# Block 0's expert numbers worked out on GpSimd, two heads at a time, with the gathers queued behind the pairs

## The reference

```python
def peer_rows(xb, w_pq, sub_keys, peer_u, peer_v):
    q = (xb @ w_pq).reshape(n, 8, 2, 128)
    s = jnp.einsum('nhcd,hckd->nhck', q, sub_keys)          # 8 heads x 2 halves x 128 keys
    top_s, top_i = lax.top_k(s, 16)
    cand_s = (top_s[:, :, 0, :, None] + top_s[:, :, 1, None, :])   # 256 sums per head
    cand_i = (top_i[:, :, 0, :, None] * 128 + top_i[:, :, 1, None, :])
    best_s, best_pos = lax.top_k(cand_s, 16)
    idx = jnp.take_along_axis(cand_i, best_pos, axis=-1)    # 16 expert rows per head
    g = jax.nn.softmax(best_s, axis=-1)
    a = jax.nn.gelu(jnp.einsum('nd,nhkd->nhk', xb, peer_u[idx]))
    return jnp.einsum('nhk,nhkd->nd', g * a, peer_v[idx])
```

## Time and profile before

| | |
|---|---|
| median of 3 runs | 2230.27 us (2228.47 to 2231.19) |
| profiled execution | 2234.23 us |
| its span | 2232.4 us |
| mean granted TensorE clock | 0.819 |
| TensorE matmul busy | 1487.6 us (67%) |
| VectorE busy | 1345.3 us (60%) |
| GpSimd busy | 1073.2 us (48%), 1126 instructions |
| ScalarE busy | 205.8 us (9%) |
| bytes moved | 748.24 MB, mean 335 GB/s |

### The profile page before, as it was taken

The page is one execution under the profiler, slowest core; times in us unless marked ns, Lnnn a source line. Parts: engine busy times, 40 slices in busy tenths (PEclk is TensorE's granted clock), DMA queues, the critical chain, the costliest instruction groups (busy, mean ns, idle before and its releaser), DMA issues.

```text
span 2232.4 us, 17911 instructions
## 1 busy us (share of the span) xinstructions
PE 1487.6 (67%) x6304; PEld 678.1 (30%) x6304; DVE 1345.3 (60%) x2853; ACT 205.8 (9%) x464; POOL 1073.2 (48%) x1126
## 2 busy tenths in 40 slices
PE   6989679988853334999923379995004995004998
PEld 3444443454641212443411123661001221001222
DVE  2778962244289775551479861476999934995001
ACT  3113300002100100001110001110000001000000
POOL 0411112110016565555545445557777777766773
PEclk9999789878876666999955599998556997556999
DMA  6777437736359998999989889999999999999997
GB/s 264 263 288 277 156 120 284 299 118 245 132 208 379 405 405 340 404 385 388 355 344 381 334 352 371 353 358 398 409 409 409 408 409 409 410 411 410 409 409 299
DMA packets 219113, 748.24 MB, mean 335 GB/s; under 512 B 20384, under 2 KB 25248, under 8 KB 208656
## 3 DMA queue, kind: packets, MB, share of 16 engines
q0 software_dynamic: 160368, 616.91, 70.9%
q1 hardware_dynamic: 50464, 121.24, 14.7%
q10 hardware_dynamic: 8192, 8.95, 1.1%
HBM read 736.98 MB, written 10.04 MB: 335 GB/s over the span
## 4 chain that ended last, share of the span: by engine, by line
PE 45%; DMA 24%; DVE 14%; POOL 9%; issue 6%; ACT 2%; ACTq 0%; SPq 0%; DVEq 0%; POOLq 0%
PE ps L1850 17%; DMA arena<-in_peer_u,arena 16%; PE ps L1633 15%; POOL arena L629 9%; DMA arena<-in_peer_v,arena 6%; DVE arena L1295 6%; PE ps L2022 4%; DVE arena L981 3%; DMA arena<-in_cache_diff_v,arena 1%; PE ps L1740 1%; PE ps L1637 1%; PE ps L1594 1%; PE ps L2012 1%; PE ps L1806 1%; PE ps L1798 1%
## 5 line engine op out<-in xcount | busy, mean ns | idle before, releaser
L629 POOL DMA_INDIRECT arena<-in_peer_u,arena x520 | 488.0, 938 | 450.7 <-DVE arena L1295 216.1
L1295 DVE CUSTOM_DVE_ANT_0 arena<-arena,ps 128x1024 f32<-128x1024 f32 x512 | 611.6, 1219 | 63.7 <-DMA arena<-in_peer_u,arena 48.3
L629 POOL DMA_INDIRECT arena<-in_peer_v,arena x520 | 495.7, 953 | 281.2 <-PE ps L1850 149.1
L1850 PE MATMUL ps<-arena 128*32 128x512 f32 x2048 | 557.7, 604 | 10.2 <-DMA arena<-in_peer_v,arena 5.3
L1633 PE MATMUL ps<-arena 128*128 128x512 f32 x960 | 440.0, 614 | 7.4 <-ACT arena L681 6.6
L1850 PEld LDWEIGHTS ps<-arena 128*32 128x32 f32 x2048 | 152.2, 110 | 382.7 <-issue 285.3
L1633 PEld LDWEIGHTS ps<-arena 128*128 128x128 f32 x960 | 184.0, 196 | 240.3 <-issue 229.8
L981 DVE TENSOR_TENSOR arena<-arena 128x256 f32<-128x256 f32 (+12 forms) x299 | 188.9, 667 | 28.7 <-ACT arena L964 8.6
L1841 PE MATMUL ps<-arena 128*128 128x128 f32 x4 | 1.6, 389 | 290.4 <-DVE arena L981 290.4
L981 DVE TENSOR_TENSOR arena<-arena,ps 128x512 f32<-128x512 f32 (+6 forms) x59 | 48.9, 831 | 213.1 <-PE ps L1633 77.0
L2022 PE MATMUL ps<-arena 128*128 128x128 f32 (+1 forms) x768 | 133.0, 330 | 2.2 <-ACT arena L681 1.4
(11 more groups left out here) (224 smaller groups left out, 1233.7 us busy)
## 6 DMA issues: line engine op xcount, KB each, us to landing
arena<-in_w_pq SPq DMA_DIRECT2D x12, 2048.0 KB, 18.8
arena<-in_w_in SPq DMA_DIRECT2D x7, 2048.0 KB, 10.9
arena<-in_w_out SPq DMA_DIRECT2D x6, 2048.0 KB, 14.8
arena<-in_w_mq SPq DMA_DIRECT2D x6, 2048.0 KB, 9.9
arena<-in_w_mo SPq DMA_DIRECT2D x6, 2048.0 KB, 19.5
arena<-in_peer_u,arena POOLq DMA_INDIRECT x520, 11.3
arena<-in_peer_v,arena POOLq DMA_INDIRECT x520, 14.1
arena<-in_cache_mem_k SPq DMA_DIRECT2D x8, 1024.0 KB, 7.0
```

The source lines that it names most:

```text
L629: return pool.indirect_dma_start(slot, None, table[0], bass.IndirectOffsetOnAxis(idx.bitcast(U32), 0))
L1295: dve.tensor_tensor_reduce(row, row, x_copy(b), 1.0, 0.0, ALU.mult, ALU.add, DOTS[:, k:k + 1]).then_inc(s["u_used"], 1)
L1850: last = pe.matmul(PS[32 * j:32 * j + 32, 6 + half, :], window(n, i, j), row[:, 512 * half:512 * half + 512], start=(n == 0 and i == 0), s ...
```

## The change

Only block 0 is concerned (`b == 0`); for the other blocks `select_heads` is as before. For block 0, VectorE stops behind the two comparisons. It writes the rows of 0 and 1 not to HOTS but to one of two buffers PAIR_HOTS in the ring, copies the pair's key numbers (64 per token) to PAIR_NUMBERS, and raises `heads_found`. From the third pair on it first waits for `picked`, so that GpSimd has done with the buffer.

GpSimd has a new function `pick_pair`: wait for `heads_found`; four multiplications; four additions that halve the 16 places to one (8, 4, 2, 1); times 128, plus the second number, and a conversion into IDX, which raises `picked` by two. Pair 0 is done before the first gather; pairs 1, 2 and 3 stand, one after another, behind the nine gathers that have a free place, and before the tenth. To make room for the two new semaphores, `new_kv_stored` and `state_stored` become one, `rows_and_state_stored`, and the wait for the state is at 16 x 10 + 16.

```diff
--- before.py
+++ after.py
@@ -268,19 +268,20 @@
...
-        mem_stored0 mem_stored1 mem_stored2 mem_stored3 new_kv_stored lam_sums lam_exp line_ps line_row
+        mem_stored0 mem_stored1 mem_stored2 mem_stored3 rows_and_state_stored lam_sums lam_exp line_ps line_row
...
@@ -452,6 +453,9 @@
         HOTS = at("t", 0, 1024)
         BV, BI, AU, CU = (at("t", 1024 + 32 * i, TOPK * HEADS) for i in range(4))
         GAC = at("t", 1296, 2 * TOPK * HEADS)
+        PAIR_HOTS = [at("ring", 1024 * i, 1024) for i in range(2)]
+        PAIR_NUMBERS = [at("t", 1360 + 64 * i, 2 * TOPK * HEADS) for i in range(2)]
+        PAIR_SUM = at("t", 1488, TOPK * HEADS)
         bsum, bmax = at("t", 1184, PH), at("t", 1192, PH)
         IDX = at("const", CW - NB * NSEL, NB * NSEL).rearrange("p (b k) -> p b k", b=NB)
         GATE = at("s", 320, NB * NSEL).rearrange("p (b k) -> p b k", b=NB)
@@ -631,12 +635,46 @@
 
             pool.wait_ge(s["mixed_turned"], NB - 1)
             pool.wait_ge(ns_stored[2], stored_through(2))
+            pool_links = [0]
+
+            def plink(ins):
+
+                pool_links[0] += 1
+                ins.then_inc(s["pool_steps"], 1)
+                pool.wait_ge(s["pool_steps"], pool_links[0])
+
+            def pick_pair(p):
+
+                wide = HEADS * TOPK
+                pool.wait_ge(s["heads_found"], p + 1)
+                hots = PAIR_HOTS[p % 2].rearrange("p (t h k a) -> p t h k a", t=2, h=HEADS, a=TOPK)
+                numbers = PAIR_NUMBERS[p % 2].rearrange("p (h t k) -> p h t k", h=HEADS, t=2)
+                for half in range(2):
+                    for h in range(HEADS):
+                        last = pool.tensor_tensor(hots[:, half, h], hots[:, half, h],
+                                                  numbers[:, h, half].unsqueeze(1).broadcast_to([P, TOPK, TOPK]), ALU.mult)
+                plink(last)
+                h3 = PAIR_HOTS[p % 2].rearrange("p (x a) -> p x a", a=TOPK)
+                n = TOPK // 2
+                while n:
+                    plink(pool.tensor_tensor(h3[:, :, 0:n], h3[:, :, 0:n], h3[:, :, n:2 * n], ALU.add))
+                    n //= 2
+                number = IDXF[:, wide * p:wide * p + wide]
+                plink(pool.tensor_scalar(PAIR_SUM, h3[:, 0:wide, 0], float(NK), None, ALU.mult))
+                plink(pool.tensor_tensor(number, PAIR_SUM, h3[:, wide:2 * wide, 0], ALU.add))
+                pool.tensor_copy(IDX[:, 0, wide * p:wide * p + wide].bitcast(U32), number).then_inc(s["picked"], HEADS)
+
             for kind, b, k0, k1 in RUNS:
                 if b == SMP and kind == "u":
                     pool.wait_ge(s["idxt_ready"], PICKS.index(SMP) + 1)
                 elif b != SMP and kind == "v":
                     pool.wait_ge(s["idxt_ready"], PICKS.index(b) + 1)
                 for k in range(k0, k1):
+                    if (kind, b, k) == ("u", 0, 0):
+                        pick_pair(0)
+                    if (kind, b, k) == ("u", 0, len(VSLOT)):
+                        for p in range(1, PH // HEADS):
+                            pick_pair(p)
                     slot, _, before = GATHERS[kind, b, k]
                     if not before and slot >= len(VSLOT):
                         pool.wait_ge(s["rqp_ready"], NSUB * LAST + (12 if slot < len(VSLOT) + 4 else 16))
@@ -738,7 +776,7 @@
                     j = first_job(kind) + b
                     take(j, dst[0:ROWS[b], b, :])
                     taken(j)
-                    act.dma_start(outs if b == SMP else outp[b], dst[0:ROWS[b], b, :]).then_inc(s["new_kv_stored"], 16)
+                    act.dma_start(outs if b == SMP else outp[b], dst[0:ROWS[b], b, :]).then_inc(s["rows_and_state_stored"], 16)
                     if kind == "dk" and b < H:
                         line_copy(b)
                 if kind == "dk":
@@ -750,7 +788,7 @@
                 act.dma_start(TOE[:, h, :], line_dram[o:o + P * (TL - 1)].rearrange("(p c) -> p c", p=P)[:, 0:512]
                               ).then_inc(s["toe_loaded"], 16)
 
-            act.wait_ge(s["new_kv_stored"], 16 * NSTORES)
+            act.wait_ge(s["rows_and_state_stored"], 16 * NSTORES)
             act.wait_ge(s["srow_saved"], 1)
             for st in range(NBLK * H + 2):
                 if st < NBLK * H:
@@ -792,7 +830,7 @@
                               SLOT[TILE_SLOT[n][0]][:, 0:512].rearrange("p (h e) -> p h e", h=H)).then_inc(ns_stored[TILE_SLOT[n][0]], 16)
             act.wait_ge(s["ret_state"], NBLK)
             act.dma_start(state_p[0, 0].rearrange("h d e -> d h e"), STATE.rearrange("p (h e) -> p h e", h=H)
-                          ).then_inc(s["state_stored"], 16)
+                          ).then_inc(s["rows_and_state_stored"], 16)
 
             def head_sqrt(n, b0, b1):
                 act.wait_ge(s["hsq_ready"], n + 1)
@@ -1145,7 +1183,7 @@
             link(tt(sself_m[0:DB], sself_m[0:DB], sself_e[0:DB], ALU.add))
             tt(colmax[0:DB, :].rearrange("p (b c) -> p b c", b=DB), colmax[0:DB, :].rearrange("p (b c) -> p b c", b=DB),
                sself_m[0:DB], ALU.max).then_inc(s["largest_ready"], 1)
-            dve.wait_ge(s["new_kv_stored"], 16 * NSTORES)
+            dve.wait_ge(s["rows_and_state_stored"], 16 * NSTORES)
             dve.wait_ge(s["av_done"], NBLK * H)
             turned_row("rq", 0, DV, 0)
 
@@ -1383,6 +1421,18 @@
                 dve.tensor_copy(GATE[0:r, b, h0 * TOPK:(h0 + HEADS) * TOPK], BV[0:r])
 
                 wide = HEADS * TOPK
+                if b == 0:
+                    p = h0 // HEADS
+                    if p >= 2:
+                        dve.wait_ge(s["picked"], HEADS * (p - 1))
+                    dve.tensor_copy(PAIR_NUMBERS[p % 2], TIFB[b][:, h0 * 32:(h0 + HEADS) * 32].bitcast(U32))
+                    for half, pos in enumerate((AU, CU)):
+                        last = tt(PAIR_HOTS[p % 2][:, 512 * half:512 * half + 512].rearrange("p (x a) -> p x a", a=TOPK),
+                                  pos.bitcast(U32).unsqueeze(2).broadcast_to([P, wide, TOPK]),
+                                  const("iota16").unsqueeze(1).broadcast_to([P, wide, TOPK]), ALU.is_equal)
+                    last.then_inc(s["heads_found"], 1)
+                    dve.wait_ge(s["heads_found"], p + 1)
+                    return
                 hots = [HOTS[0:r, 512 * half:512 * half + 512] for half in range(2)]
                 iota = const("iota16")[0:r].unsqueeze(1).broadcast_to([r, wide, TOPK])
                 for hot, pos in zip(hots, (AU, CU)):
@@ -1428,7 +1478,7 @@
             for g, blocks in enumerate(GROUPS):
                 prompt = [b for b in blocks if b != SMP]
                 if g == 0:
-                    dve.wait_ge(s["state_stored"], 16)
+                    dve.wait_ge(s["rows_and_state_stored"], 16 * NSTORES + 16)
                     head_norm(1, 1, NBLK, SQ)
                     dve.wait_ge(s["x_again"], 32)
                 residual("mix", g)
```

More of the change, by code:

```diff
@@ L275 @@
         ret_sc_ready ret_out ret_state ret_rows rqm_ready kexp_ready outer_ready ns_ready ns_stored0 ns_stored1
[L276 to L283, removed]
+        ns_stored2 hsq_ready hrstd_done mix_ready x_again done_stored final_ready mkr_loaded mkr_turned mkT_done
+        mv_loaded cs_ready cmax_ready cexp_done ce_turned ceT_ready co_ready co_taken cqb_ready cs_scored
+        ccolmax_turned cmaxbc_ready csexp_done cesum_ready cz_ready ccoef_ready cpv_done com_ready crow_ready
+        sk_loaded sk_turned skT_done rqp_ready rqp_taken rs_ready rs_taken xb_ready gelu_done weight_ready
+        y_ready u_used v_used select_steps picked idx_turned idxt_ready gate_arg gate_exp_done gates_done
+        w_turned wx_ready slot_in0 slot_in1 slot_in2 slot_in3 slot_in4 slot_in5 slot_in6 slot_in7 slot_in8
+        slot_in9 slot_in10 slot_in11 slot_in12 slot_in13 slot_in14 slot_in15 slot_in16 qdec_loaded sq_stored
+        qb_in0 qb_in1 mixed_turned mixed_done tile_in3 largest_ready clargest_ready x_in_ps heads_found
+        pool_steps""".split()
 def build(nc, x_prompt, x_sample, mem_prompt, cache_diff_k, cache_diff_v, page_table, state_ret, cache_mem_k,
```

## The result

The changed kernel takes 2217.85 us in the median of seven runs (2213.41 to 2224.75) against 2228.47 us before (median of seven; the forecast started from the first three, 2230.27, and said 2221.8): ratio 0.9951, interval 0.9937 to 0.9965. Measured again on the chip of the last experiments it took 2220.39 us, ratio 0.9959 (0.9943 to 0.9975). That is 10.6 and 9.1 us faster by the medians; forecast were 8.5. The profiled execution took 2216.49 us, its span is 2214.7 us, 17.7 less than before. Half of that lies ahead of the change: the fourth sort of block 0's router began at 600.03 instead of 609.00, and how much of it is more than scatter between executions stays open (first experiment).

What follows compares the result with a forecast made beforehand. No single engine was the bound; TensorE, DMA and VectorE shared the chain, with VectorE nearly full in block 0's selection. -11.9 + 3.5 = -8.4, taken as 8.5, off the 2230.27 median gave 2221.8 us; range 2215.5 to 2229.5.

Steps and rivals of the forecast that it cites:

- VectorE's path: Block 0's router and selection: 2.98 us net off VectorE per pair, four pairs, 11.9 us in all.
- rival 1: Block 0's router: TensorE keeps its clock, both stalls go, gain 11.7 or up to 14 us; chance 0.18.
- the first stall: VectorE's 1.62 us wait for TensorE's matmuls after pair 0; forecast to keep its size if the clock still falls.
- GpSimd's pair: GpSimd's eleven instructions with seven waits per pair in block 0, taken as 7.5 us between bounds 3.5 and 13.9.
- rival 3: Block 0's sorts, gates, first dot products: VectorE held while GpSimd computes; at half speed 6.5 us slower, 2237; chance 0.10.
- The lag behind pair 3: Tenth gather waits for GpSimd's pair 3, so gathers move 8.4 us, not 11.9; VectorE meets 3.5 us in full.
- The sum -11.9 + 3.5 = -8.4: Block 0's path: VectorE's shorter selection less the gathers' lag behind pair 3; 8.5 us gain taken.
- the collision: The DMA-limited stage behind selection: w_mq tiles move by 8.9 us, gathers by 8.4, so the full stretch begins that much earlier.
- The damping: Stage behind selection: with a 13.9 us pair, the second w_mq tile fills part of the gap; about 5 us gain left.
- X: GpSimd's time for one pair's arithmetic in block 0, forecast 7.5 us.

Runs made afterwards that it cites:

- the last experiments: Changed kernel with group 1's first w_mq tile issue held until VectorE's first dot product is done, 2224.05 us; changed kernel with pair 1 behind six gathers, 2219.53 us.
- first experiment: The kernel before with only the merged semaphore rows_and_state_stored added: 2230.43 us, ratio 1.0002.
- the seven traces with GpSimd's arithmetic: Changed kernel, profiled twice (2217.85, 2220.39 us), and its five variants: last pair on VectorE, last pair late, longer pair 3, w_mq held, pair 1 sooner (2219.53 to 2224.48 us).
- pair 3 late: Changed kernel with pair 3 moved behind 64 gathers in GpSimd's queue and the numbers' transpose moved to behind the first mo job: 2223.35 us, ratio 0.9978.
- w_mq experiment: Changed kernel with SyncE's issue of group 1's first w_mq tile held until VectorE's first dot product is done: 2224.05 us, ratio to before 0.9976.
- the longer pair: Changed kernel with five more GpSimd additions of 128x512 between pair 3 and the tenth gather: 2224.48 us, ratio 0.9978.

## Why the prediction held, and where its reasoning did not

- **VectorE's path, -11.9 forecast, -11.15 measured.** Stretch by stretch, from sort to sort, to pair 3's selection and to the first dot product: 18.03 to 15.05, 18.04 to 13.99, 18.05 to 16.44, 12.50 to 9.99. The first is the forecast 2.98. The second gained 1.1 more, the third 1.4 less (the held sums of pair 2), the fourth 0.5 less.
- **TensorE's clock (rival 1).** I took no gain, and little or nothing of one reached the path. At the first stall, after 4.62 us of idle time, the 16 matmuls still took 3.41 us, as at the lower level in the earlier trace rows, and VectorE's stall stayed at 1.62. At the second, after 3.93 us of idle time, they took 2.68, and the stall fell from 1.61 to 0.57 us. Over the seven traces with GpSimd's arithmetic these idle times of 3.91, 3.93, 4.12, 4.13, 4.16, 4.17 and 4.29 us go with 2.65, 2.68, 3.05, 3.07, 3.11, 3.15 and 3.38 us. But in the six of them with pair 1 behind nine gathers, VectorE's sums behind this stall, which began 30.7 to 31.2 us behind the fourth sort, all ended at 32.9: GpSimd's additions set their end. What the clock gave in the second stretch is part of what the third lost.
- **GpSimd's pair, 7.5 forecast, 7.4 to 7.5 measured, in part by luck.** VectorE's durations of 3.5 us plus eleven times 0.30 gave 6.8. As far as the rough spans of GpSimd tell, both terms were off in pair 0, in opposite ways. The eleven instructions were busy for 6.6 us (the multiplications 2.8, which took VectorE 1.44; the additions 3.0, where I had 1.5; the last three 0.8), and the pauses came to 0.8 us, most of them 0.08 and not 0.30. The Trainium skill's figure ("GPSIMD Engine Reference", Performance versus the Vector engine) gave an estimated 4.6 us of work and, with turnarounds, about 7; the trace agrees with this total and not with its parts.
- **The engines in each other's way (rival 3)** is real and small: 1.4 us at the candidate sums, 0.43 at the gates' subtraction (0.72 against 0.29), nothing at the sorts (0.30 throughout). The Trainium skill's rule ("SBUF — State Buffer", The single rule) lets GpSimd's arithmetic meet only VectorE instructions with two SBUF inputs or in a two-port mode, and the one that starts later is held; the trace agrees. The one-input sorts ran on. The gates' later multiplication, with two inputs, began at 654.57 and kept its 0.29, and GpSimd's multiplication, begun at 654.60, took 0.86 instead of 0.73. I had applied the rule to the gates and overlooked the candidate sums of pair 2, since I had not laid pair 1, shifted by nine gathers, over VectorE's list.
- **The lag behind pair 3, 3.5 forecast, 3.4 measured (3.68 us behind the first dot product, where it was 0.28); that VectorE "meets the lag of 3.5 us in full" was wrong.** This is the step that failed. VectorE did wait (2.06 + 0.39 us), but by the 33rd gather nothing was left of it, and without the lag (pair 3 late) the same gather came within 0.1 us of the same place. The sum -11.9 + 3.5 = -8.4 reached its value by the wrong road, and that is luck. What carried the gain is the stretch that I had named as the collision: it starts with TensorE's w_mq tile, three pairs behind the start, forecast -8.9, measured -9.1, and the 65th dot product is 9.5 ahead. The w_mq experiment and the counts of bytes show it. Both roads gave nearly the same number, so the time alone could not tell them apart.
- **The damping** for a long pair ("about 5 us would be left" at X = 13.9) is near what the longer pair showed at X = 7.5 + 5.2 = 12.7: 162.4 - 157.0 = 5.4 us left at the 65th dot product, with the tenth gather only 2.5 us ahead.

Open: why TensorE restarted the more slowly the longer it had been idle, and why the router began sooner in all seven traces. Also not tried: more landing places for block 0, which would fill the DMA's empty time before the w_mq tile.

## What to carry to other kernels

Where a stage behind runs at the DMA's limit, find the transfer with which its full stretch begins, wanted or not, and see what releases it: lags of other transfers are free while that one fills the time, and a late one costs though nobody waits for it. Before moving arithmetic to GpSimd, lay its new schedule, shifted by what stands ahead in its queue, over VectorE's instructions with two SBUF inputs. When two chains give the same forecast, move one of them alone before believing the reason.

## What I had not expected of the hardware

GpSimd's pause of 8.7 us in full flow, with nine landing places, was only partly covered by the gathers in flight (2.5 us lost), while a lag of 3.7 us at the start of the stretch cost nothing. Beside GpSimd's arithmetic VectorE's sorts showed no delay, but two sums of 128x256 took 2.16 us instead of 0.76.
